# Finding the first expert's rows without the lists, and building the job table beside its products

## The chip, the cores and the metric

The kernel runs on one core of one Trainium2 chip. The metric is the device time of one launch in microseconds, taken as the median of several runs. The profile is of one further execution.

## What is computed

One decoder layer for 512 prompt rows and 8 sample rows, 1024 wide: an input projection, three mixers (pooling, dilated attention, a convolution), an output projection and a layer norm, then a mixture of 32 experts of which each row takes four, and a second layer norm. The part that matters here:

```python
logits = jnp.einsum('md,de->me', xt, router_w, ...) + router_b
top_v, top_i = lax.top_k(logits, TOP_K)          # 4 of 32
gates = jax.nn.softmax(top_v, axis=-1)
...
def run_block(args):                             # rows of one expert
    hh = xblk @ e_w_in[e] + e_b_in[e]
    gate, up = jnp.split(hh, 2, axis=-1)
    ...
    act = gate * jax.nn.sigmoid(SWIGLU_ALPHA * gate) * (up + 1)
    return act @ e_w_out[e] + e_b_out[e]
```

and the sum of the results per row, weighted by the gates. All is float32.

## The kernel before, in words

`layer` runs two blocks one after the other; each block ends with a barrier of all engines, and each has its own program for SyncE, GpSimd, ScalarE, TensorE (PE) and VectorE.

**first_block** does everything up to the router. The prompt rows are four tiles of 128, worked in the order 3, 2, 1, 0 (`TILES`), and the sample rows are a fifth tile, NT, which comes first (`NTH` is the place of a tile in that order). `AFTER` is an order written out by hand: which product of which tile stands at which step of the attention. For each tile VectorE normalises the rows (`shifted1`, `scaled1`), ScalarE stores them to `x1_dram` and `acc_dram` (`x1_store`, L759), PE computes the logits (`logits`), VectorE takes the four best experts (`choose_experts`, called by `route`) into the 0/1 table `memb`, PE counts with 0/1 products how many earlier rows chose the same expert (`rank`), and VectorE turns the rank into a place (`place_in_lists`, L1438). GpSimd scatters row number and gate to that place in `lists_dram` (`list_rows`, L656, four indirect DMAs a tile). After the last tile VectorE builds the job table from the totals (`job_table`, L1566, with two rounds through PE: `placed_ready` to `ordered`, and `fields_ready` to `fields_turned`) and writes it to `jobs` (`job_rows`, L1613). When all scatters have landed (`listed`), SyncE and ScalarE load the lists to SBUF (L622 to L626, L840 to L842). Then the block ends.

**moe_block** works off jobs. A job is up to five groups of 32 rows of one expert; the most frequent expert comes first but for expert 0, which a constant puts ahead of all. Expert weights stream through `ring`, twelve slots of 1 MB: eight hold the up and gate weights, four the down weights. The slots of expert 0 are loaded in first_block. In moe_block SyncE loads the next expert's unit k into its slot as soon as the product that reads it is done (`load_unit`, L278; `wait_ge(up_done, ...)`, L1727 on). For each job GpSimd gathers the rows (`gather`, L1776), VectorE turns them (`turn_rows`, L2000), PE does `up` (L1856) and, one job later, `down` (L1874), VectorE and ScalarE the activation, ScalarE `results` (L1935), and GpSimd scatters the results with an addition onto `acc_dram` (`scatter`, L1785). VectorE's `name_rows` (L1989) takes a job's gates and indices from the lists, which the gather needs; for jobs 0, 1 and 2 it stands ahead of the loop, with memsets of the PSUM tiles `pu` and `py` (L2014, L2015). At the end GpSimd waits for all scatters and signals `sums_done` (L1838), on which SyncE loads the sums for the second layer norm (L1748).

## Time and profile before

| what | us |
|---|---|
| median of 3 runs (lowest, highest) | 1352.47 (1349.94, 1352.83) |
| the profiled execution | 1353.31 |
| its span, first to last instruction | 1351.5 |
| PE busy | 1180.6 (87%) |
| VectorE busy | 515.6 (38%) |
| ScalarE busy | 272.9 (20%) |
| GpSimd busy | 244.6 (18%) |
| mean GB/s over the span | 343 |
| mean granted TensorE clock | 0.952 |

The span ends with the last instruction; the 1.8 us around it belong to the launch. Shares of busy time are means over stages with different limits: first_block ends at about 286 us, and moe_block takes the rest. The page shows the span in 40 slices of 33.8 us. In a timeline a line stands for neighbouring instructions of one kind; the time in brackets is how long the engine was idle before it, with what ended that. "issue" is time in which the engine waited for nothing that the profile shows. PEld is the load of weights into the array, SPq, ACTq and POOLq are the sequencers that issue DMAs.

### The profile page before, as it was taken

To read this page: it belongs to the slowest core of one execution; us is meant where nothing else is said; L and a number is where in the kernel's file an instruction comes from. 1 tells how busy PE (TensorE), PEld (TensorE's weight loads), DVE (VectorE), ACT (ScalarE), POOL (GpSimd) and SP (SyncE) were. 2 spreads that over 40 slices of the span, in tenths; PEclk is the share of its full clock that TensorE was granted. 3 is DMA by queue.
4 is the path that set the end of the run, shared out by engine and by line. 5 is a ranking of instruction groups with operands and counts; after the bars stand their busy time and mean duration, and the time that the engine had idled before them with its cause. 6 is when DMAs were issued, how large, how long until landed. Compare 5 with 4: busy or idle time off the path is not lost.

```text
span 1351.5 us, 34174 instructions
## 1 busy us (share of the span) xinstructions
PE 1180.6 (87%) x12540; PEld 521.5 (39%) x12541; DVE 515.6 (38%) x875; ACT 272.9 (20%) x533; POOL 244.6 (18%) x214
## 2 busy tenths in 40 slices
PE   7998999836999999999899989989898989998750
PEld 6886545512333333433233333433333333433210
DVE  2997637854232222232324141421323220422226
ACT  0003234400102230141121211130121210132212
POOL 4000001431111221142121311221121212130112
PEclk9999999958899999999999999999999999999765
DMA  9702931649999999999999999999999999999943
GB/s 356 201 3 97 289 146 34 261 152 414 416 419 411 409 413 381 419 385 413 417 410 416 409 413 413 409 404 418 416 407 415 410 419 363 409 403 422 412 177 128
DMA packets 79976, 463.18 MB, mean 343 GB/s; under 512 B 12324, under 2 KB 20873, under 8 KB 29709
## 3 DMA queue, kind: packets, MB, share of 16 engines
q1 hardware_dynamic: 69083, 438.76, 80.3%
q0 software_dynamic: 8768, 17.47, 5.1%
q10 hardware_dynamic: 2066, 6.32, 1.2%
q8 instruction: 18, 0.29, 0.1%
q14 instruction: 41, 0.34, 0.1%
HBM read 447.51 MB, written 19.48 MB: 346 GB/s over the span
## 4 chain that ended last, share of the span: by engine, by line
PE 51%; DMA 21%; issue 3%; DVE 2%; ACT 0%; DVEq 0%; ACTq 0%; POOLq 0%; SPq 0%; POOL 0%
PE pu L1866 32%; PE rest L1880 17%; DMA ring<-in_e_in 15%; DMA ring<-in_e_out 6%; PE pu L1860 1%; PE rest L1891 1%; DVE fin L2082 0%; DVE bn L2064 0%; DVE xgT L2003 0%; DVE mv L2075 0%; PE rest L1885 0%; ACT y L1946 0%; DMA fin<-acc_rows 0%; DVE idx L1995 0%; ACT fin L1977 0%
## 5 line engine op out<-in xcount | busy, mean ns | idle before, releaser
L1866 PE MATMUL pu<-ring,xgT 128*32 128x512 f32 x5248 | 587.6, 601 | 37.8 <-DMA ring<-in_e_in 37.1
L1866 PEld LDWEIGHTS pu<-ring,xgT 128*32 128x32 f32 x5248 | 162.2, 111 | 445.3 <-issue 444.7
L1880 PE MATMUL rest<-ring,hid 128*32 128x256 f32 x5248 | 301.5, 387 | 20.1 <-DMA ring<-in_e_out 11.8
L2033 DVE TENSOR_SCALAR gg<-pu 128x1280 f32<-128x1280 f32 x32 | 47.7, 1492 | 607.2 <-PE pu L1866 607.2
L1789 POOL DMA_INDIRECT acc_rows<-y,row x82 | 110.7, 1350 | 748.0 <-ACT y L1946 731.8
L1880 PEld LDWEIGHTS rest<-ring,hid 128*32 128x32 f32 x5248 | 168.4, 112 | 143.0 <-issue 41.3
L1946 ACT ACTIVATE y<-rest,gate 32x256 f32 x328 | 152.8, 466 | 292.8 <-issue 289.1
L1926 ACT ACTIVATE ss<-gg 128x1280 f32<-128x1280 f32 x32 | 40.7, 1272 | 540.5 <-DVE gg L2033 540.5
L866 PE MATMUL pair<-xt,ring 128*128 128x260 f32 x448 | 101.7, 389 | 6.9 <-DMA ring<-in_w_in 5.8
L1779 POOL DMA_INDIRECT xq<-x_rows,idx x82 | 88.2, 1075 | 90.0 <-issue 78.2
L866 PEld LDWEIGHTS pair<-xt,ring 128*128 128x128 f32 x448 | 86.4, 194 | 21.0 <-DMA xt<-in_xT 6.8
L1210 DVE SCALAR_TENSOR_TENSOR conv<-conv,chan_sb 128x512 f32<-128x512 f32 x90 | 67.7, 752 | 3.1
L1860 PE MATMUL pu<-brow,chosen 128*32 128x512 bf16 x328 | 25.8, 413 | 40.9 <-issue 29.3
L2003 DVE STREAM_TRANSPOSE xgT<-xq 128x1280 f32<-128x1280 f32 x33 | 49.7, 1506 | 0.0
L2045 DVE TENSOR_TENSOR uu<-uu,ss 128x1280 f32<-128x1280 f32 x32 | 47.7, 1492 | 1.1
L2050 DVE STREAM_TRANSPOSE hid<-uu 128x1280 f32<-128x1280 f32 x32 | 48.1, 1504 | 0.0
L2048 DVE CAST chosen_down<-cst 128x32 bf16 x32 | 5.8, 181 | 109.7 <-PE rest L1880 106.8
L2043 DVE SCALAR_TENSOR_TENSOR uu<-uu,gg 128x1280 f32<-128x1280 f32 x32 | 47.6, 1486 | 0.0
L2035 DVE TENSOR_SCALAR uu<-pu 128x1280 f32<-128x1280 f32 x32 | 47.4, 1481 | 0.0
L662 POOL DMA_INDIRECT list_rows<-pairs,spots x20 | 21.1, 1055 | 126.1 <-DVE spots L1453 121.6
L1003 PE MATMUL pair<-ring,mix 128*128 128x512 f32 x80 | 39.7, 647 | 0.0
L1860 PEld LDWEIGHTS pu<-brow,chosen 128*32 128x32 bf16 x328 | 6.8, 99 | 60.0 <-issue 57.9
(270 smaller groups left out, 542.3 us busy)
## 6 DMA issues: line engine op xcount, KB each, us to landing
ring<-in_e_in SPq DMA_DIRECT2D x256, 1024.0 KB, 23.9
ring<-in_e_out SPq DMA_DIRECT2D x128, 1024.0 KB, 25.1
ring<-in_w_in SPq DMA_DIRECT2D x3, 1536.0 KB, 24.5
ring<-in_w_in SPq DMA_DIRECT2D x5, 512.0 KB, 11.0
ring<-in_w_o SPq DMA_DIRECT2D x1, 2048.0 KB, 12.0
conv<-in_x_prompt SPq DMA_DIRECT2D x1, 2048.0 KB, 13.8
x_rows<-conv ACTq DMA_DIRECT2D x4, 512.0 KB
acc_rows<-conv ACTq DMA_DIRECT2D x4, 512.0 KB
```

Source lines behind the costliest of these rows:

```text
L866: mm = nc.tensor.matmul(b[:, h, 0:HALF], wtile[:, tiles_of(lo, lo + P).start, k], xt[:, k, h * HALF:(h + 1) * HALF], start=k == 0, stop=k ...
L1210: ch.mark(V.scalar_tensor_tensor(cy[:, i, 0:SEQ], u[:, i, t:t + SEQ], taps[:, i, t:t + 1], cy[:, i, 0:SEQ], ALU.mult, ALU.add))
L1779: nc.gpsimd.indirect_dma_start(out=xq[:, u % 2, j], out_offset=None, in_=x1_quarters, in_offset=bass.IndirectOffsetOnAxis(ap=idx4[:, u % A ...
L1789: nc.gpsimd.indirect_dma_start(out=acc_dram, out_offset=bass.IndirectOffsetOnAxis(ap=row4[0:GS, u % AHEAD, j:j + 1], axis=0), in_=y[at, u ...
L1866: mm = nc.tensor.matmul(pu[quarter(c), j], xgT[:, j, k], w[:, :, c * QC:(c + 1) * QC], start=False, stop=k == KT - 1, skip_group_check=True)
L1880: mm = nc.tensor.matmul(py[quarter(c), j], hid[:, j, 2 * q + f], w[:, f, c * QC:(c + 1) * QC], start=False, stop=q == FT // 2 - 1 and f == ...
L1946: ins = nc.scalar.activation(y[to, bass.ds(u % 2, 1), j // NQ, c * QC:(c + 1) * QC].rearrange("p o n -> p (o n)"), py[of, j], ACT.Copy, sc ...
L2003: V.transpose(xgT[:, :, :, :].rearrange("p j k s -> p (j k s)"), xq[:, half].rearrange("p j n -> p (j n)")).then_inc(turned, 1)
L2033: V.tensor_scalar(gg[:, :, :], pu[:, :, 0], SW_LIMIT, None, ALU.min).then_inc(g_ready, 1)
L2043: at.do(V.scalar_tensor_tensor(uu[:, :, :], uu[:, :, :], 1.0, gg[:, :, :], ALU.add, ALU.mult))
L2045: V.tensor_tensor(uu[:, :, :], uu[:, :, :], ss[:, :, :], ALU.mult).then_inc(h_ready, 1)
L2050: V.transpose(hid[:, :, :, :].rearrange("p j f s -> p (j f s)"), uu[:, :, :].rearrange("p j n -> p (j n)")).then_inc(hid_ready, 1)
```

## The change

The lists, job table and expert stream are as they were, but the first job no longer needs them.

- **The first expert's rows.** For every tile VectorE makes a 0/1 table of row against slot, `in_slot`, from the rank for expert 0 (`first_slots`, two operations). PE multiplies it with the row numbers, split in two bf16 parts (`first_ids_of`): 80 products for the tiles NT, 3, 2 and 1, ahead of `logits(0)`, and 20 for tile 0 behind the totals. VectorE adds the two and writes the first job's indices `idx4[:, 0]`, and the first job's size `first_size` from the totals. GpSimd gathers the rows (`gather_first`) within first_block, after a wait for all stores of the rows. `next_expert` tells SyncE which expert follows.
- **What moves.** The scatter of tile 0's list entries goes from the end of first_block to the head of moe_block; the loads of the lists go to ScalarE's queue in moe_block (eight loads); the rest of `job_table` and `job_rows` go to VectorE in moe_block, behind `turn_rows(0)`, and the four products that turn the fields stand in the middle of the first `up` (`turn_fields`). `jobs_ready` is a new semaphore on which SyncE, GpSimd, ScalarE, PE and VectorE wait before they read `jobs` or `count`. PE's first `up` stands ahead of its loop.
- **Memory.** `pu`, `rest`, `pairs`, `spots`, `idx4`, and `qkv` (under which `xq`, `xgT` and `hid` now lie) belong to both blocks. The PSUM memsets go to VectorE's head in first_block, with a wait on PE's first use of each bank. The zero fills of `xq` on ScalarE and GpSimd go, since the memory holds finite numbers. Small tables move into `cpre`, which is free by then.
- **The end.** SyncE waits for the count of scatters itself; `sums_done` goes.

The core of the diff:

```diff
@@ first_block, gpsimd
-            for i in (NT,) + TILES:
+            for i in (NT,) + TILES[:-1]:
                 list_rows(i, NTH[i])
+            gp.wait_ge(x1_sent, 32 * (NT + 1))
+            gp.wait_ge(first_named, 1)
+            size = gp.value_load(first_size[0:1, 0:1], min_val=1, max_val=JG)
+            x1_quarters = x1_dram.rearrange("r (c n) -> (r c) n", n=QC)
...
+            gather_first(0)
@@ first_block, tensor
+            def first_ids_of(tiles, dst):
+                pe.wait_ge(slots_ready, NTH[tiles[-1]])
+                for j in range(JG):
+                    for i in tiles:
+                        m = rows(i)
+                        for c in range(NQ):
+                            mm = nc.tensor.matmul(dst[c * GS:(c + 1) * GS, j], in_slot[0:m, i, j * GS:(j + 1) * GS],
+                                                  id_parts[0:m, i], start=i == tiles[0], stop=i == tiles[-1],
+                                                  skip_group_check=True)
+                mm.then_inc(ids_done, 1)
...
             turn_rows1(0)
+            pe.wait_ge(s_max, 2 * NSTEPS)
+            first_ids_of((NT,) + TILES[:-1], ids_early)
             logits(0)
             rank(0)
-            pe.wait_ge(s_max, 2 * NSTEPS)
...
+            pe.wait_ge(ids_kept, 1)
+            first_ids_of((0,), ids_last)
@@ first_block, vector
+            for b in pair:
+                V.memset(b[:, :, :], 0.0).then_inc(psum_zero, 1)
+            for b in bS + bT:
+                ch.mark(V.memset(b[:, :], 0.0))
...
+            def first_slots(i, ranks):
+                m = rows(i)
...
+                ch.do(V.scalar_tensor_tensor(keys[0:m, i:i + 1], ranks[:, 0:1], 1.0, memb[0:m, i, 0:1], ALU.add, ALU.mult))
+                V.tensor_scalar(in_slot[0:m, i], C("slot", m), keys[0:m, i:i + 1], None, ALU.is_equal
+                                ).then_inc(slots_ready, 1)
...
             scaled1(1)
+            d.wait_ge(ids_done, 1)
+            V.tensor_copy(early_ids[:, :, :], ids_early).then_inc(ids_kept, 1)
             root1(0)
             shifted1(0)
             route(0)
             scaled1(0)
+            d.wait_ge(rank_done, NTH[0] - 1)
+            d.wait_ge(m_ready, NTH[0])
+            first_slots(0, ranks_of(0))
...
+            V.tensor_scalar(idx4[:, 0], first_ids[:, :, 0], float(NQ), C("quarterpad"), ALU.mult, ALU.add
+                            ).then_inc(first_named, 1)
@@ moe_block, sync
-            first = expert_of(1)
+            first = sp.value_load(next_expert[0:1, 0:1], min_val=0, max_val=NE - 1)
...
+            sp.wait_ge(jobs_ready, 1)
...
-            sp.wait_ge(sums_done, 1)
+            done = sp.value_load(jobs[0:1, 4, bass.ds(last, 1)], min_val=1, max_val=JG * MAXJ)
+            sp.wait_ge(scattered, 16 * done)
@@ moe_block, scalar
-            nc.scalar.activation(xq[:, 0]...).then_inc(xq_zero, 1)
+            a.wait_ge(listed, 16 * TOPK * (NT + 1))
+            for c in range(NQ):
+                a.dma_start(lists[c * GS:(c + 1) * GS, 0:NE * JG], lists_dram[:, 0:NE * JG]).then_inc(lists_in, 16)
+            for c in range(NQ):
+                a.dma_start(lists[c * GS:(c + 1) * GS, NE * JG:], lists_dram[:, NE * JG:]).then_inc(more_lists_in, 16)
@@ moe_block, vector
+            choose(0)
+            turn_rows(0, d.value_load(first_size[0:1, 0:1], min_val=1, max_val=JG))
+            job_table()
+            job_rows()
+            d.wait_ge(jobs_ready, 1)
             d.wait_ge(lists_in, 16 * NQ)
             name_rows(ch, 0, 0)
-            choose(0)
-            ch.mark(V.memset(pu[:, :, :, :], 0.0))
-            ch.mark(V.memset(py, 0.0))
             d.wait_ge(more_lists_in, 16 * NQ)
             for u in (1, 2):
                 name_rows(ch, u, d.value_load(jobs[0:1, 2, u:u + 1], min_val=0, max_val=NE * MAXN - 1))
-            turn_rows(0, through(slice(1, 2)))
```

## Rows read from the trace of the kernel before

**Rows 1.** the page, slices of 33.8 us: DMA share, GB/s.

```profile
DMA  9702931649999999999999999999999999999943
GB/s 356 201 3 97 289 146 34 261 152 414 416 419 411 409 413 381 419 385 413 417 410 416 409 413 413 409 404 418 416 407 415 410 419 363 409 403 422 412 177 128
```

**Rows 2.** window: PE, PEld, DVE, ACT, POOL busy us; granted clock, DMA share, GB/s.

```profile
1200.00:1250.00 50.00, 44.47 (x550) 16.36 (x542) 18.26 (x22) 10.00 (x18) 4.18 (x5) 1.00 1.02 415
```

**Rows 3.** DMA issues: queue, count, KB each, us to landing.

```profile
ring<-in_e_in SPq DMA_DIRECT2D x256, 1024.0 KB, 23.9
...
rw<-in_router_w ACTq DMA_DIRECT2D x1, 128.0 KB, 21.2
...
l2b<-in_ln_b SPq DMA_DIRECT2D x1, 512.0 KB, 16.3
```

**Rows 4.** timeline (start us, us, engine, line), the stream's start.

```profile
294.74 1.04 PE L1860 MATMUL pu<-brow,chosen 128*32 128x512 bf16 x8 [11.57 <-DVE xgT L2003]
...
298.70 12.31 SPq L281 DMA_DIRECT2D ring<-in_e_in  x8
...
318.69 7.92 SPq L281 DMA_DIRECT2D ring<-in_e_in  x8
```

**Rows 5.** the columns of rows 2, in the gap.

```profile
278.00:280.00 2.00, 0.00 (x0) 0.00 (x0) 1.77 (x16) 0.00 (x0) 0.99 (x2) 0.50 0.10 30
```

**Rows 6.** timeline, a PSUM memset and PE's first product.

```profile
287.32 2.19 DVE L2014 MEMSET pu<- 128x2560 f32 x1 [0.53 <-issue]
...
5.59 3.81 PE L866 MATMUL pair<-xt,ring 128*128 128x260 f32 x8 [5.59 <-DMA ring<-in_w_in]
```

**Rows 7.** timeline, VectorE from last projection to job fields.

```profile
262.70 1.28 DVE L1411 TENSOR_TENSOR conv<-conv,pair 128x512 f32<-128x512 f32 x2
...
268.43 0.25 DVE L1418 SCALAR_TENSOR_TENSOR lg<-route_sums,mv,pair 128x32 f32<-128x32 f32 x1
...
275.70 0.19 DVE L1581 COPY xt<-bS 128x32 f32<-128x32 f32 x1 [0.77 <-PE bS L1181]
...
281.04 0.21 DVE L1610 TENSOR_SCALAR xt<-xt 128x1 f32<-128x1 f32 x1
```

**Rows 8.** the columns of rows 2, in the attention part.

```profile
200.00:250.00 50.00, 48.68 (x255) 27.24 (x254) 36.75 (x129) 19.29 (x59) 7.54 (x8) 1.00 0.22 77
```

**Rows 9.** timeline, grouped form and window: small products.

```profile
264.88 1.94 PE L1052 MATMUL pair<-rw,xt 128*128 128x32 f32 x16 [0.18 <-ACT xt L797]
...
270.89 0.42 PE L1174 MATMUL bS<-memb,tri_bf 128*32 128x32 bf16 x5
...
L1174 PE MATMUL bS<-memb,tri_bf 128*32 128x32 bf16 x4 | 0.3, 193 | 0.0
...
270.00:272.00 2.00, 1.08 (x15) 0.84 (x15) 1.93 (x5) 0.00 (x0) 0.00 (x0) 0.57 1.00 268
```

**Rows 10.** timeline, the last store of the rows.

```profile
272.07 0.95 ACTq L763 DMA_DIRECT2D acc_rows<-conv  x1
```

**Rows 11.** timeline and window, gathers to the first turn.

```profile
286.17 1.27 ACT L1952 ACTIVATE xq<-cst 128x1280 f32<-128x1280 f32 x1 [16.37 <-PEq L325]
...
288.36 1.06 POOL L1779 DMA_INDIRECT xq<-x_rows,idx  x1 [9.06 <-ACT xq L1952]
...
290.00:292.00 2.00, 0.00 (x0) 0.00 (x0) 2.00 (x7) 0.00 (x0) 1.63 (x2) 0.50 0.29 78
...
292.33 1.51 DVE L2003 STREAM_TRANSPOSE xgT<-xq 128x1280 f32<-128x1280 f32 x1
```

**Rows 12.** timeline, chain and window at the stream's end.

```profile
1316.35 1.32 POOL L1789 DMA_INDIRECT acc_rows<-y,row  x1 [8.94 <-ACT y L1946]
...
1318.97 3.05 issue
...
1323.99 2.14 SPq L1714 DMA_DIRECT2D fin<-acc_rows  x5
...
1318.00:1319.00 1.00, 0.00 (x0) 0.00 (x0) 0.00 (x0) 0.00 (x0) 0.00 (x0) 0.50 0.28 37
```

342 lines of the change are left out of this document (198 added, 144 removed).

## The prediction

> **What bounds the kernel now.** I read the page's slices first. From the ninth slice (270 to 304 us) on, the DMA row stands at 9 and the GB/s row near 412 until the last two slices [rows 1]. A stretch of 50 us says the same more finely: DMA share 1.02 at 415 GB/s, while PE is busy 44 of 50 us [rows 2]. What is streamed is fixed: the page's list of DMA issues gives 256 units of 1 MB for the up weights, eight per expert [rows 3], and the down weights are four more per expert, 384 in all. The first expert's twelve come before this stretch; the other 372 need a slot that a product has emptied. So the kernel is: a first part that ends with the first unit of expert products, then a saturated stream whose length is bytes over rate, then a tail. What moves the start of the stream moves its end by as much, as long as the stream never runs dry; what makes an engine faster inside it is worth nothing.
>
> Next I read the place where the stream starts. PE begins the first up product at 294.74, SyncE issues its first unit at 298.70 (3.96 later), and the next eight units at 318.69 [rows 4]. [...]
>
> **Parts with one answer.** The PSUM memsets move to the head of VectorE: 2560 columns took 2.19 us, 0.86 us per thousand, so 4096 columns cost some 3.6 us from 0.3 to 4 us; PE's first product starts at 5.59, held by its DMA [rows 6]. Nothing, with 1.6 us to spare; without that cover it would cost up to 3.6. The zero fills of xq on ScalarE and GpSimd go: worth nothing of their own, as the path is built anew below. The two operations of first_slots for each of the tiles NT, 3 and 2 (some 0.5 us a tile, twice the 0.25 of L1418 [rows 7]) lie beside PE, which is busy 48.68 of 50 us where VectorE is busy 36.75 [rows 8]; between 0 and 1.5, I take 0.3. The constants grow by 171 columns (88 KB) and no early wait is on them.
>
> **The front, step by step.** From PE's last projection on, VectorE leads. I shift the old times.
> 1. first_slots(1) stands ahead of rest_sum(0), which started at 262.70: +0.5. turn_rows1(0) on PE, done at 264.7, is done at 265.2 [rows 7].
> 2. 80 new products (5 groups, 4 tiles, 4 quarters) of 32 weight columns and 2 moving columns stand on PE ahead of logits(0). The nearest row is L1174, five products of 32 weight columns in 0.42 us; one alone takes 0.19, so each further one 0.055 [rows 9]. 80 x 0.055 = 4.4, so 269.6. Bounds: 0.19 each (15.2 us), if none overlaps, and 0.028 each (2.2 us), if the spacing halves with the clock, which was granted at 0.57 in that window [rows 9]. I take the row as it stands.
> 3. logits(0) took 1.95 [rows 9]: 271.55. VectorE copies the early numbers and runs root and shift (1.3) beside it. route(0) starts at 271.65 and not at 268.43: +3.2 [rows 7].
> 4. scaled1(0) ended at 271.67, now 274.9. first_slots(0) 0.5, 20 products 1.2, three chained operations 0.65: the indices of the first expert are there at 277.4.
> 5. GpSimd first waits for the stores of x1 and acc_rows. The last was issued at 272.07 (0.95 long) [rows 10]; now 3.2 later, until 276.2. With it the DMA engines were busy until 278 and fell to 30 GB/s then [rows 5]; a store issued until 276.2 lands at 279.0 by my choice (bounds 277.5, where the old ones had ended, and 281). This wait ends later than step 4, so it is the one that decides.
> 6. GpSimd starts a gather 0.9 after its releaser (ScalarE's fill ended at 287.44, the gather started at 288.36), and the second follows 1.36 later: 279.9 to 282.3. In the old kernel the gathered bytes moved within 290:292, right behind the issues [rows 11]; landed by 283.5.
> 7. The block ends with GpSimd. VectorE ended at 285.36 and its first operation of the next block was at 286.33: +1.0, 283.3. Its memset, choose and one value load take 1.0, the turn of the rows 1.5, PE's start 0.9 (293.84 to 294.74) [rows 4, 11]: PE starts at 286.7 and not at 294.74. **Front: -8.0** (bounds -10.0 and +5.4, by steps 2 and 5). VectorE's other work ahead of the block's end (tables, weigh, place: 1.3 + 2.1 + 0.4 after 277.4) ends at 281.2, 1.1 before GpSimd; that is its cover.
>
> **What is moved behind the start.** The job table takes 275.70 to 281.25 [rows 7]; it now starts at 285.8 and its fields are there at 291.3. PE has four units behind it at 295.6 (the old first up ended at 310.47 and the last four of its eight units took 6.9, so they began 8.9 after its start; 286.7 + 8.9), so it does not wait; the four turning products add 1.9 us (281.31 to 283.17), jobs_ready is at 299.6, and the first up ends at 304.4. Queued behind: the four list scatters of tile 0, 4 x 1.29 after 283.3, landed at 289.7; then eight loads on ScalarE's queue, issued until 293.2. They land within 2 us in a quiet machine (issued 280.50 to 283.24, the bytes gone by 285); with SyncE's queue full a small load on ScalarE's queue took 21.2 (rw, at the start of the kernel) [rows 3]. I take 5: VectorE is at name_rows until 303.1, the second job's gather lands near 307, and VectorE can turn it at 304.4 + 3.0. The second up starts 5.7 after the first ends, as before, at 310.1, its first unit is issued at 312.6, 21.9 us after the stream's first (before: 20.0). The queue holds eight units and the LN2 rows, which were issued at 311.53 and landed 16.3 later [rows 3], 29.1 us after the first issue. The stream has 7.2 us of slack there and nothing is lost, save the bytes: 640 KB of lists (four loads of 40 KB, four of 120) now share the stream, 0 to 1.6 us at 412 GB/s; I take **+1.0**.
>
> [...]
>
> **The tail.** The last scatter is issued at 1316.35 (1.32 long). GpSimd then walks out of its unrolled loop: the chain shows two long stretches of "issue", the second of 3.05 us, and SyncE's first load of the sums is at 1323.99. The DMA windows have the scatter's bytes in 1318:1319 [rows 12] and almost nothing after 1320. With SyncE waiting on the scatters itself, it starts at about 1320.1: **-3.9** (bounds -5.5 and 0). Late next is nothing new: ScalarE's table was loaded at 1316.78, and GpSimd's first addition is wanted only at 1328.8.
>
> **Sum.** -8.0 + 0.3 + 1.0 - 3.9 = -10.6. The profiled execution took 1353.31 (span 1351.5), so 1342.7; it lies 0.84 above the median of 1352.47, so 1341.9 for a median.
>
> **Rivals.**
> - More gain (0.16): products at 0.028 us, stores landed at 277.5 and the other steps of the front a little shorter give -10.0, a scatter landed by 1318.5 gives -5.5, the lists nothing: 1337.3. For it: the clock is at its upper level when the 80 run; against it that other rows of this width have the same spacing at that level (54 products of L1880 in 3.23 us, though of 256 columns).
> - The lists come late (0.12). If the eight loads take the 21.2 us of rw, they land at 314, the second job's rows are turned at 321 and the stream's next issue is at 33.8 us, 4.7 after the queue is empty: 1346.6.
> - The tail gives nothing, since the accumulating scatter's own completion is what took until 1323 (0.12): 1345.8. For it: the chain cannot show when a semaphore was raised. Against it: the bytes.
> - The start moves but not the end, since some later stage refills the gap (0.05): only the tail is left, 1348.6. Against it the share of 1.0 throughout.
> - Slower (0.04): the small products do not overlap. At 0.19 us each, 100 of them cost 19 us where I have 5.6, all of it ahead of the router and of the x1 stores: +13.4 - 10.6 = +2.8, 1355.3 for a median. The sum turns at 0.16 us a product.
> - The change does what it says by its code; I give no case to the contrary.
>
> **How the numbers follow.** Forecast 0.51, 1340 to 1344.5. To hold 8 in 10 the range takes in the larger gain and the two middle losses: 1337 to 1348. A measurement of this kernel tells 0.2% (2.7 us) from no change. Faster by more: forecast, more gain, lists, tail and most of the fourth case, 0.92. Within 0.2%: 0.04, the fourth case with a small loss. Slower: 0.04.
>
> **What would show it.** In the profile after: the first up product near 286.7, SyncE's first unit near 290.7; 80 products in about 4.4 us and logits(0) behind them; GpSimd's first gather near 279.9, released by a DMA and not by VectorE; the first up with a pause of about 2 us in its middle; DMA share 1.0 without a hole 25 to 35 us after the first unit; SyncE's loads of the sums some 2.5 us after the last scatter's issue and not 6.3. The prediction is wrong if the stream has a hole there, if the gather waits for something later than the stores, or if the new products take 0.1 us or more.

## The result: slower by 0.3%

The changed kernel took 1355.7 us as the median of 14 runs (1353.57 to 1360.36), the kernel before 1352.8 us on the same chip: a ratio of 1.003, with a 95% interval of 1.0019 to 1.0042. The forecast was faster by 10.6 us. In the profiled executions the spans are 1352.3 us after and 1351.5 before. Here and below, a difference in us is the ratio times the median of the kernel before, and intervals go the same way; the two medians can lie apart by another amount, here by 2.9 us where the ratio says 4.1. Two executions of the kernel with the tail change alone, at 2484.76 and 1444.74 us, count as slow and stand in no ratio.

The page after, the rows that answer to [rows 1] (DMA share and GB/s of 40 slices), and the windows that answer to [rows 2] and [rows 5], with one more in a place that becomes important:

```profile
DMA  9703930749999998999999999999999999999953
GB/s 356 203 3 111 298 124 34 272 168 403 415 418 412 408 412 330 417 376 411 418 409 415 410 412 413 407 409 412 416 408 414 410 418 383 392 406 420 412 221 128
```

```profile
278.00:280.00 2.00, 0.00 (x0) 0.00 (x0) 0.00 (x0) 0.00 (x0) 0.00 (x0) 0.50 0.00 0
520.00:540.00 20.00, 20.00 (x219) 6.51 (x215) 2.23 (x2) 0.70 (x1) 0.00 (x0) 1.00 0.76 282
1200.00:1250.00 50.00, 46.59 (x574) 17.34 (x566) 18.25 (x22) 7.67 (x13) 6.92 (x6) 1.00 1.02 410
```

The sixteenth slice stands at 330 GB/s where it was 381: a hole in the stream. In 520:540 it is 282 GB/s, where the kernel before moved 371, and PE is busy in all 20 us, within a job of 320 products. The waits of PE in the changed kernel (engine, line, what for: us in total, times, longest), first all of those in 370:620, then the longest group in 620:1310:

```profile
PE pu L1882 <- issue: 7.9, 8, 1.8
```

```profile
PE pu L1888 <- DMA ring<-in_e_in: 34.8, 34, 2.2
```

Up to 620 us PE never waits for a load of weights (in the kernel before twice, 1.1 us in all). Behind that it does, again and again.

The front of the changed kernel, as a timeline (start, duration, engine, line, operation, idle time before it and what ended that):

```profile
263.92 1.47 PE L1045 MATMUL pu<-cpre,ktok 8*32 8x2 bf16 x80
265.32 3.49 PE L1095 MATMUL pu<-rw,xt 128*128 128x32 f32 x16
268.91 0.25 DVE L1464 SCALAR_TENSOR_TENSOR cpre<-cpre,mv,pu 128x32 f32<-128x32 f32 x1 [1.15 <-PE pu L1095]
...
272.56 0.45 ACTq L797 DMA_DIRECT2D acc_rows<-conv  x1
...
273.57 0.23 DVE L1637 TENSOR_SCALAR idx<-cpre,cst 128x5 int32<-128x5 f32 x1
...
280.53 1.06 POOL L698 DMA_INDIRECT qkv<-x_rows,idx  x1 [11.92 <-issue]
...
286.35 0.18 DVE L2028 CAST chosen<-cst 128x32 bf16<-128x32 f32 x1 [9.03 <-PEq L346]
...
289.39 1.04 PE L1882 MATMUL pu<-brow,chosen 128*32 128x512 bf16 x8 [13.64 <-DVE qkv L2044]
...
293.64 0.35 SPq L301 DMA_DIRECT2D ring<-in_e_in  x1
```

So the start did move: PE's first up product from 294.74 to 289.39 and SyncE's first unit from 298.70 to 293.64 [rows 4], 5.1 to 5.4 us earlier. Then the head start is lost. The second and third up product of the changed kernel:

```profile
307.58 0.17 DVE L2034 COPY gate<-lists 128x5 f32 x1 [5.47 <-DMA lists<-list_rows]
...
309.55 1.05 POOL L1801 DMA_INDIRECT qkv<-x_rows,idx  x1 [18.01 <-DVE idx L2036]
...
315.81 1.51 DVE L2044 STREAM_TRANSPOSE qkv<-qkv 128x1280 f32<-128x1280 f32 x1 [0.79 <-DMA qkv<-x_rows,idx]
...
318.13 0.62 PE L1882 MATMUL pu<-brow,chosen 128*32 128x512 bf16 x4 [11.60 <-DVE qkv L2044]
318.52 8.67 PE L1888 MATMUL pu<-ring,qkv 128*32 128x512 f32 x56
330.21 1.86 PE L1888 MATMUL pu<-ring,qkv 128*32 128x512 f32 x8 [3.02 <-issue]
...
347.95 0.83 PE L1882 MATMUL pu<-brow,chosen 128*32 128x512 bf16 x12
```

and the same of the kernel before:

```profile
316.16 0.62 PE L1860 MATMUL pu<-brow,chosen 128*32 128x512 bf16 x4 [5.69 <-issue]
316.56 9.53 PE L1866 MATMUL pu<-ring,xgT 128*32 128x512 f32 x64
...
343.00 1.51 PE L1860 MATMUL pu<-brow,chosen 128*32 128x512 bf16 x12
```

The second up product starts 2.0 us later than before instead of 5.4 earlier, and takes until 332.1 with a pause of 3.02 us ahead of its last eight products; the third starts 4.95 us later. VectorE reads the first product at 312.04, 5.5 us after it ended; in the kernel before it does so at once. The last scatter's issue is 4.5 us later too (1320.84 against 1316.35 [rows 12]), and the tail gives about that back:

```profile
1320.84 1.31 POOL L1811 DMA_INDIRECT acc_rows<-y,row  x1 [9.95 <-ACT y L1984]
1324.27 2.60 SPq L1734 DMA_DIRECT2D fin<-acc_rows  x5
```

SyncE loads the sums 3.43 us after the scatter's issue where it took 7.64 [rows 12].

Two theories go into the experiments. **P**: TensorE's chain, from the second up product to about 615 us, decides, and the stream has slack until then; the hole at 520 us is where its head start goes. **S**: the stream's start decides, as forecast. What made the second and third up products late is a question of its own, with three suspects: the lists, the second job's gather, and TensorE's code.

### The profile page after: what moved, and what is told of

The parts are those of the page before. It is cut to its first block, busy times and chain, and to the rows that moved or that the text cites. A ratio compares the mean times of both kernels' runs of the same rounds, so it can differ in the third digit from the quotient of the medians.

```text
span 1352.3 us, 34408 instructions
## 1 busy us (share of the span) xinstructions
PE 1182.7 (87%) x12640; PEld 524.3 (39%) x12641; DVE 519.2 (38%) x900; ACT 271.9 (20%) x532; POOL 242.8 (18%) x213
## 4 chain that ended last, share of the span: by engine, by line
PE 50%; DMA 23%; issue 3%; DVE 2%; ACTq 0%; ACT 0%; DVEq 0%; POOL 0%; SPq 0%; POOLq 0%
PE pu L1888 31%; PE rest L1904 16%; DMA ring<-in_e_in 14%; DMA ring<-in_e_out 8%; PE pu L1882 1%; DMA lists<-list_rows 1%; PE rest L1915 1%; DVE fin L2185 0%; DMA qkv<-x_rows,idx 0%; DVE bn L2167 0%; DVE mv L2178 0%; DMA fin<-acc_rows 0%; DMA acc_rows<-y,row 0%; DMA list_rows<-pairs,spots 0%; PE rest L1909 0%
## 5 line engine op out<-in xcount | busy, mean ns | idle before, releaser
L1888 PE MATMUL pu<-ring,qkv 128*32 128x512 f32 x5248 | 592.9, 605 | 38.1 <-DMA ring<-in_e_in 34.8
L1888 PEld LDWEIGHTS pu<-ring,qkv 128*32 128x32 f32 x5248 | 165.1, 111 | 445.8 <-issue 442.8
L1904 PE MATMUL rest<-ring,qkv 128*32 128x256 f32 x5248 | 299.2, 386 | 17.0 <-DMA ring<-in_e_out 11.0
L1904 PEld LDWEIGHTS rest<-ring,qkv 128*32 128x32 f32 x5248 | 167.6, 111 | 139.3 <-issue 35.5
L898 PE MATMUL pu<-xt,ring 128*128 128x260 f32 x448 | 101.1, 388 | 7.8 <-DMA ring<-in_w_in 6.0
L1801 POOL DMA_INDIRECT qkv<-x_rows,idx x80 | 86.2, 1077 | 95.1 <-issue 64.9
L898 PEld LDWEIGHTS pu<-xt,ring 128*128 128x128 f32 x448 | 85.9, 192 | 21.8 <-DVEq L1239 5.2
L2044 DVE STREAM_TRANSPOSE qkv<-qkv 128x1280 f32<-128x1280 f32 x33 | 49.7, 1506 | 1.7 <-issue 0.9
L2153 DVE STREAM_TRANSPOSE qkv<-uu 128x1280 f32<-128x1280 f32 x32 | 48.2, 1505 | 0.0
L1035 PE MATMUL pu<-ring,mix 128*128 128x512 f32 x80 | 39.7, 647 | 0.0
```

The lines of the kernel that those rows point to most:

```text
L898: mm = nc.tensor.matmul(b[:, h, 0:HALF], wtile[:, tiles_of(lo, lo + P).start, k], xt[:, k, h * HALF:(h + 1) * HALF], start=k == 0, stop=k ...
L1801: nc.gpsimd.indirect_dma_start(out=xq[:, u % 2, j], out_offset=None, in_=x1_quarters, in_offset=bass.IndirectOffsetOnAxis(ap=idx4[:, u % A ...
L1888: mm = nc.tensor.matmul(pu[quarter(c), j], xgT[:, j, k], w[:, :, c * QC:(c + 1) * QC], start=False, stop=k == KT - 1, skip_group_check=True)
L1904: mm = nc.tensor.matmul(py[quarter(c), j], hid[:, j, 2 * q + f], w[:, f, c * QC:(c + 1) * QC], start=False, stop=q == FT // 2 - 1 and f == ...
L2044: V.transpose(xgT[:, :, :, :].rearrange("p j k s -> p (j k s)"), xq[:, half].rearrange("p j n -> p (j n)")).then_inc(turned, 1)
L2153: V.transpose(hid[:, :, :, :].rearrange("p j f s -> p (j f s)"), uu[:, :, :].rearrange("p j n -> p (j n)")).then_inc(hid_ready, 1)
```

## Experiment: the tail alone, and the front alone

```diff
+            done = sp.value_load(jobs[0:1, 4, bass.ds(last, 1)], min_val=1, max_val=JG * MAXJ)
+            sp.wait_ge(scattered, 16 * done)
-            sp.wait_ge(sums_done, 1)
...
-            gp.sem_inc(sums_done, 1)
```

> The kernel before with nothing but the change in the tail: SyncE waits for the two scatters of the row sums itself, and GpSimd's own signal is gone. In the changed kernel the load of the sums was issued 3.43 us after the last scatter's issue, against 7.64 us before. If that saving is one of the wait's form, this kernel has it too and is 4.2 us faster than the kernel before (about 1348.6 us). If the scatter's own landing set the 7.64 us, or if the saving only swallows a wait of later work, it is within 0.5 us of the kernel before.

Measured: ratio 0.9942 (0.9919 to 0.9965), 7.8 us, more than expected. The same kernel was run again, and with it the changed kernel with the old tail:

> The kernel before with the tail change alone, once more: its ratio was 0.9942 (0.9919 to 0.9965), 7.8 us, where its profile shows 4.2 us. If the 4.2 us are all, the ratio comes out near 0.9969; if there is more in it, near 0.994 again.

Measured: 0.9968 (0.9955 to 0.9982), 4.3 us. In its profile the last scatter is issued at 1315.60 and the load of the sums at 1318.89, 3.29 us later.

> The changed kernel with the old tail: GpSimd signals SyncE that the scatters are done. If the profiles size the parts rightly (tail -4.2 us, front +4.5 to +7 us), it is 4.2 us slower than the changed kernel and 7 us slower than the kernel before, near 1360 us, and the load of the sums is issued 7.6 us after the last scatter's issue again. If the tail alone is worth the 7.8 us that its kernel showed by the clock of whole runs, it is 10 to 12 us slower than the kernel before.

Measured: 1.0057 (1.0037 to 1.0077), 7.7 us slower than the kernel before. Its profiled execution was the fastest of its six runs (1354.36 us, median 1358.73), and has the scatter at 1317.70 and the load at 1325.37: 7.67 us, the old tail. The medians are only 4.8 us apart, so the size of this loss is the least certain of the three.

So the halves are: **tail -4.3, front +7.7 us** against forecasts of -3.9 and -6.7. They add up to +3.4, and +0.3% is +4.1. The first measurement of the tail alone, from five executions, was high, as the second and the profiles say. The rest is about the front.

## Experiment: the stream starts later

```diff
@@ moe_block, sync, the first eight units
-                sp.wait_ge(up_done, k + 1)
+                sp.wait_ge(up_done, min(k + 3, KT))
```

> The changed kernel, with the first eight loads that SyncE issues of the weight stream put behind one more of TensorE's up products each than they wait for now, so that the stream starts about 4 us later. Theory P (TensorE's chain from the second up product to about 615 us decides, and the stream has slack): the holes of the stream between 500 and 550 us shrink by about what it starts later, and the time is within 0.5 us of the changed kernel. Theory S (the stream's start decides, as the prediction said): about 3.7 us slower than the changed kernel, some 1359 us.

Measured: 1353.56 us, ratio 0.9999 (0.9987 to 1.0012), where the changed kernel had 1.003: not slower, but faster by some 4 us (by the medians against the kernel before, 2.7). The first unit is issued at 297.41 and not at 293.64. The window at the hole:

```profile
520.00:540.00 20.00, 20.00 (x243) 7.33 (x239) 5.38 (x8) 1.27 (x1) 0.00 (x0) 1.00 0.92 363
```

The hole has shrunk from 282 to 363 GB/s. Theory S is refuted: 3.8 us taken from the stream's start cost nothing. That it gained was not expected by either theory. The trace shows where: with less of the stream under way (208 GB/s in 296:300 where the changed kernel moved 375), the list loads of 120 KB land 3.2 us after their issue and not 8.3, VectorE's wait for the second part of the lists is 1.39 us and not 5.47, and the second up product starts at 314.89 instead of 318.13.

```profile
303.83 0.17 DVE L2034 COPY gate<-lists 128x5 f32 x1 [1.39 <-DMA lists<-list_rows]
```

## Experiment: row names ahead of the second part of the lists

```diff
-            d.wait_ge(more_lists_in, 16 * NQ)
             for u in (1, 2):
                 name_rows(ch, u, ...)
+            d.wait_ge(more_lists_in, 16 * NQ)
             ch.wait()
```

The wait is VectorE's.

> The changed kernel, with GpSimd's... and TensorE's wait for the second part of the job lists moved behind the row names of jobs 1 and 2, whose entries for these rows lie in the part that lands first. The names of job 1 then no longer wait the 5.47 us for lists. Theory P (TensorE's chain from the second up product decides): the second up product starts about 4.3 us earlier (near 313.8 instead of 318.1 us) and the time is about 4.3 us below the changed kernel's, near 1351.4 us. Theory S (the stream decides): the second up product is earlier and the time is unchanged.

Measured: 1353.93 us, ratio 0.9999 (0.9985 to 1.0013), again some 4 us below the changed kernel. The second up starts at 313.75; but the first started 2.3 us earlier in this execution (287.12), so that the distance between the two shrank only from 28.74 to 26.63 us. The names of job 1 are there at 300.9 and its gather is issued at 302.42, 7.1 us earlier; GpSimd goes on at 310.06, 6.6 us after it was through with the issue, and VectorE turns the rows at 311.53. But VectorE is not free of the lists. The wait that was moved now stands ahead of its first read of the product, which ended at 304.1:

```profile
308.57 1.49 DVE L2136 TENSOR_SCALAR gg<-pu 128x1280 f32<-128x1280 f32 x1 [6.76 <-issue]
```

The view of the loads of the second part (L1994) names who waited for them:

```profile
  DVE gg L2136: 6.8, 1
```

The last of these loads has landed at 305.38, and the chain has four lines of VectorE's sequencer (DVEq, from 305.38 to 308.15) ahead of 308.57. From 308.57 to the turn at 311.53 VectorE is never idle, and the gather has landed before it. So the lists are one cause of the loss, this edit takes only a part of it away, and the gather stands right behind them. A kernel in which VectorE reads the first product ahead of this wait was not tried.

## Experiment: only TensorE's first up product written out

```diff
@@ moe_block of the kernel before, tensor
+            size = pe.value_load(jobs[0:1, 5, 0:1], min_val=1, max_val=JG)
+            pe.wait_ge(turned, 1)
+            pe.wait_ge(chosen_ready, 1)
+            pe.wait_ge(pu_read, 1)
+            up(size, 1)
             last = job_count(pe)
...
+                    with pe.If(step > 1):
-                    with pe.If(step <= last):
+                        with pe.If(step <= last):
```

> The kernel before, with the code of TensorE's first up product written out ahead of the loop, as the changed kernel has it, so that the loop's own up code runs first for the second job. No operation is added or removed. Theory of code that is met for the first time: the second up product shows the pause of about 3 us that the changed kernel has inside it (327.19 to 330.21), takes 12.5 to 14 us instead of 9.9, and the kernel is 2.5 to 3 us slower than before. Rival (the pause comes from the data of the second job, or from elsewhere): second up as before, time within 0.5 us.

Measured: 1360.09 us, ratio 1.0043 (1.0027 to 1.0059), 5.8 us slower than before, twice what was expected, with every operation the same. This is a cause that the prediction did not have at all. The timeline of the profiled execution, which was the slowest of its twelve (1362.8 us):

```profile
317.91 0.62 PE L1860 MATMUL pu<-brow,chosen 128*32 128x512 bf16 x4 [7.06 <-issue]
318.54 4.44 PE L1866 MATMUL pu<-ring,xgT 128*32 128x512 f32 x24
324.69 3.19 PE L1866 MATMUL pu<-ring,xgT 128*32 128x512 f32 x25 [1.71 <-issue]
330.54 1.92 PE L1866 MATMUL pu<-ring,xgT 128*32 128x512 f32 x15 [2.66 <-issue]
...
352.05 1.22 PE L1860 MATMUL pu<-brow,chosen 128*32 128x512 bf16 x12
```

The second up product has two pauses, of 1.71 and 2.66 us, and takes 14.5 us from bias to end instead of 9.9. The pauses are put down to "issue": PE waited for nothing that the profile knows.

The DMA tables of narrow windows show packets beside them. The profile lists a queue `q8` of the kind "instruction", with packets of 16 KB: 18 in the whole kernel before (0.29 MB), 21 in the changed one and 21 here (0.34 MB). Stepping through in windows of 1 us, packets of this queue stand in 318:319, 330:331, 337:338 and 342:343 in the kernel before, and in 319:320, 322:323, 327:328, 334:335, 341:342 and 347:348 here. Those of 322:323 and 327:328 stand where the two pauses above begin (322.98 to 324.69 and 327.88 to 330.54), and the two long ones of the down product behind them (3.53 us until 336.49, 3.16 until 349.68) have one inside. In the changed kernel packets stand in 321:322, 327:328, 333:334 and 340:341, and its pauses are from 327.19 to 330.21, 335.06 to 336.27 and 338.74 to 342.72. The kernel before has such pauses too, in its first down product, 2.73 us until 333.15 and 3.68 until 339.58, each with one of the packets named; what the written-out copy adds are those in the second up product. Not every packet goes with a pause: those of 318:319 before, 319:320 here and 321:322 in the changed kernel have none beside them. Two stretches around the second up product, 318:332 of the changed kernel and 316:330 of the kernel before, as sums by queue kind:

```profile
q8 instruction: 2, 0.03, 0.9%
```

```profile
q8 instruction: 1, 0.02, 0.5%
```

The author's reading is that with the first up product in the loop PE's second one runs code that was read for the first, and that written out ahead it leaves the loop's own copy to be read when the stream is running (407 GB/s in 322:331 here). That `q8` carries TensorE's code is inferred from the agreement in time alone; the profile names no engine for it.

## Experiment: the same code, but no stream beside it

```diff
@@ the kernel of the last experiment, sync, head of the loop over u
+                with sp.If(u < 2):
+                    sp.wait_ge(down_done, FT)
```

> The kernel before with the first up product written out ahead of the loop, and SyncE holds the loads of the third up product until the first down product is done, so that from about 320 us, when the second's loads have landed, no transfer of the stream runs. If the pauses in the second up product and in the first down product (2.66, 3.53 and 3.16 us in the same kernel with the stream) come from reading new code behind the stream's transfers, those behind 320 us fall under 1.5 us each. If reading new code takes this long on its own, they stay at 2.5 to 3.7 us. The total says nothing here: the third up product waits for its loads.

Measured, in the one execution of this kernel:

```profile
324.39 5.25 PE L1870 MATMUL pu<-ring,xgT 128*32 128x512 f32 x40 [1.64 <-issue]
...
331.72 3.66 PE L1884 MATMUL rest<-ring,hid 128*32 128x256 f32 x64 [1.60 <-issue]
335.74 2.78 PE L1884 MATMUL rest<-ring,hid 128*32 128x256 f32 x42 [0.35 <-issue]
338.85 1.50 PE L1884 MATMUL rest<-ring,hid 128*32 128x256 f32 x22 [0.33 <-issue]
```

From 330 to 340 us the DMA share is 0.02. The packets of `q8` are there as well (in 329:330, 333:334, 336:337 and 339:340), but the three waits of the down product, 3.53, 0.70 and 3.16 us with the stream, are 1.60, 0.35 and 0.33 without. Two are as expected and the first is 0.1 us above the bound of 1.5. So the long pauses fit the reading of new code behind the stream's transfers, and most of their length is the stream's. The pause of 1.64 us in the up product still lay beside it (324.39; the DMA share in 320:330 is 0.63).

## Experiments: the first up product back in the loop

The first try puts the first job's size into the loop's first word ahead of the job table, leaves the first two passes of the loop empty, and puts `turn_fields` behind a condition in the loop's up code:

```diff
-            size = pe.value_load(first_size[0:1, 0:1], ...)
...
-            up(size, 1, turn_fields)
-            pe.wait_ge(jobs_ready, 1)
-            last = job_count(pe)
             with pe.Fori(0, NWORD) as w:
+                with pe.If(w > 0):
+                    pe.wait_ge(jobs_ready, 1)
                 word = pe.value_load(jobs[0:1, 0, bass.ds(w, 1)], ...)
                 with pe.Fori(0, 3) as i:
-                    step = 3 * w + i + 1
+                    step = ((3 * w + i + 62) & 63) + 1
```

> The changed kernel with TensorE's first up product back in the loop: its size stands in the loop's first word ahead of the job table, the transposes of the job table stand behind a condition inside the loop's up code, and the guards read the sizes. The same products run; only where their code lies is changed, besides two branches for each job. Theory C (code met for the first time while the weight stream runs costs pauses of about 3 us): the second up product takes about 9.5 us instead of 13.9, the third starts 4 to 4.5 us earlier (near 343.5 us against 347.95), and the time is about 4 us below the changed kernel's, near 1351.5 us. Rival (the pause belongs to the second job's data or the late row names): second up as in the changed kernel, time within 1 us of it.

Measured: 1361.77 us, ratio 1.0069 (1.0048 to 1.009), a miss by 10 us, and an instructive one:

```profile
301.82 1.04 PE L1883 MATMUL pu<-brow,chosen 128*32 128x512 bf16 x8 [23.65 <-issue]
...
326.23 0.62 PE L1883 MATMUL pu<-brow,chosen 128*32 128x512 bf16 x4 [7.72 <-DVE qkv L2044]
326.63 9.77 PE L1889 MATMUL pu<-ring,qkv 128*32 128x512 f32 x64
```

The second up product is as it should be (9.77 us, no pause). But PE's first product is 12.4 us late. Some 2.2 us of it were there before the passes (the first of the 80 small products stands at 266.16 and not at 263.92), and PE's wait ahead of the up product is 10.0 us longer (23.65 against 13.64): the empty passes jump over all of the up and down code, and packets of `q8` stand in 291:292, twice in 294:295 and in 299:300 before it starts. The kernel with early row names besides came out likewise:

> Both repairs of the changed kernel: first up product back in the loop, and the row names of jobs 1 and 2 ahead of the wait for the second part of the lists. If the two losses are separate (late names 4.3 us, new code 4 us), the second up product starts near 314 us and the third near 340 us, 3 us before the kernel before's 343.0; with the tail's 4.2 us and the third up product's lead this gives 1345 to 1347 us. If they overlap, the third starts near 343 us and the time is about 1349 us.

1.0091 (1.0066 to 1.0117), and with the later stream besides:

> As the kernel with both repairs, and the first eight loads of the weight stream about 4 us later. Theory P (TensorE's chain decides and small transfers of the second job suffer from the stream): the second up product starts 1 to 3 us earlier than without, the time is the same or up to 2 us less. Theory S (the stream's start decides once TensorE is early enough): 2 to 4 us more than without.

1.0117 (1.0081 to 1.0153). Both rest on a first up product near 290 and say nothing on their own question; they started it at 299.99 and 298.15.

The second try starts the inner loop at the first job's pass and works out the step number once:

```diff
-                with pe.Fori(0, 3) as i:
-                    step = ((3 * w + i + 62) & 63) + 1
+                with pe.Fori(word >> 12, 3) as i:
+                    step = pe.snap(((3 * w + i + 62) & 63) + 1)
```

> As the first kernel with the up product back in the loop, without its two empty passes ahead of the first up product (the inner loop now starts at the pass of the first job) and with the step number worked out once for each job. In that kernel TensorE sat 23.65 us ahead of its first product and not 13.64, and 2.1 to 2.3 us instead of 0.6 us ahead of each later up product. If the empty passes (jumps over code that was never read) made the first and the repeated arithmetic the second, then the first up product starts near 289.4 us again, the later ones after about 0.6 to 0.8 us, the second up product has no pause (9.8 us), the third starts near 343 to 344 us and the time is 3 to 5 us below the changed kernel's, near 1351.5 us. If a jump of about 3 us stays, the first up product starts at 292 to 293 us.

Measured: 1353.76 us, ratio 1.0003 (0.9991 to 1.0015), 0.27% below the changed kernel. The first half came out to the microsecond:

```profile
288.95 1.04 PE L1883 MATMUL pu<-brow,chosen 128*32 128x512 bf16 x8 [13.58 <-DVE qkv L2044]
...
317.75 9.52 PE L1889 MATMUL pu<-ring,qkv 128*32 128x512 f32 x64
...
341.18 1.47 PE L1883 MATMUL pu<-brow,chosen 128*32 128x512 bf16 x12 [0.62 <-issue]
```

No packet of `q8` moves between 317 and 327 (the changed kernel had one in 321:322), and the third up product starts 6.8 us earlier than in the changed kernel. But the next eight jobs give 5.7 us back: from the end of the third up product to the up product near 600 us it takes 238.6 us (363.53 to 602.14), against 232.9 in the changed kernel (369.37 to 602.23) and 231.9 before (365.52 to 597.40). The loss stands at every third job: 2.2 to 2.3 us ahead of the up product instead of 1.6 to 1.8, and 22.5 us for 192 products instead of 20.8.

With the early row names besides:

> The same with the row names of jobs 1 and 2 ahead of the wait for the second part of the lists. Second up product near 314 us, third near 339 to 341 us. With the tail's saving this gives 1345 to 1348 us if each loss is separate; if the third up product is held by the pauses of the first down product, as in the kernel before, it is 1348 us, the time of the kernel with the tail change alone.

Measured: 0.9982 (0.9967 to 0.9997). Its front started late in the profiled execution (290.40), and the third up product at 340.90.

What the loss at every third job is, was asked with two more:

```diff
-                with pe.If(w > 0):
-                    pe.wait_ge(jobs_ready, 1)
+                pe.wait_ge(words_ready, w + 1)
```

> As the loop kernel with early row names, and the condition at each word of the loop (two branches) replaced by a wait on a counter that is always met later. In that kernel the wait ahead of every third up product was 2.2 to 2.3 us against 1.6 to 1.8 in the changed kernel, and the up product behind it took 22.5 us instead of 20.8 (192 products) and 35.7 instead of 34.5 (320 products). If the condition's jump makes these, they return to 1.7, 20.8 and 34.5 us, eight jobs take 233 us again instead of 238.6, and the time is 4 to 5 us lower, near 1346.5 us. If the place of the code in the instruction memory makes them, they stay, or move to other jobs, and the time changes by under 2 us.

Measured: 1348.73 us, ratio 0.9969 (0.9956 to 0.9982). The wait is 1.9 us, the 320 products take 34.51 again, the 192 behind the first backward jump 21.92, and the eight jobs 235.9 us: a part of the loss goes with the condition, not all of it. VectorE still waits here for the second part of the lists, ahead of its first read of the product:

```profile
309.71 1.49 DVE L2137 TENSOR_SCALAR gg<-pu 128x1280 f32<-128x1280 f32 x1 [6.89 <-issue]
```

```diff
-            with pe.Fori(0, NWORD) as w:
+            with nc.Fori(0, NWORD, engines=OrderedEngineSet([pe.engine]), hint_back_edge=True) as w:
```

> The same with the option of the outer loop that announces its backward jump. [...]

Measured: 0.9987 (0.9974 to 1.0001): no gain; the wait is 2.1 to 2.2 us, the 192 products are back at 20.81, and the 320 take 35.93. Between 380 and 600 us no packet of `q8` moves in any of these kernels, so if those packets are TensorE's code, this loss is not the reading of it. What it is stays open.

## Experiment: the code at another place

```diff
@@ the changed kernel with early row names, tensor
-            with pe.Fori(0, NWORD) as w:
+            with nc.Fori(0, NWORD, engines=OrderedEngineSet([pe.engine]), head_slot={pe.engine: 0}) as w:
```

> [...]

Measured: 1353.96 us, ratio 1.0006 (0.9993 to 1.0018). In the kernel with early row names, without the option, the second up product has its pauses after 32 and 56 products (0.78 and 2.96 us) and the first down product after 26 and 64 (0.54 and 3.78). The places moved: the first up product has a pause of 0.95 us now, PE sits 13.56 us ahead of the second (it starts at 321.06 and then runs 9.70 us without a pause), and the down product's pauses of 2.24, 1.86 and 2.39 us stand ahead of its bias, after 32 and after 96 products. The products and their data are the same, so the pauses do not belong to the data. That they go with the code's place is what is left; no view shows where the code lies.

## Experiment: a condition around each job

```diff
@@ the kernel before, tensor, in the loop
+                    with pe.If(step > 0):
-                    with pe.If(step <= last):
+                        with pe.If(step <= last):
```

> The kernel before with one more condition, always true, around what TensorE does for each job, as the changed kernel has it. The wait ahead of each up product should grow by the 0.12 us by which it is longer in the changed kernel (1.77 against 1.66 us, 0.64 against 0.52 us), so that eight jobs between 366 and 600 us take 232.9 instead of 231.9 us. Theory C expects no new pause inside the second up product and at most 1 us on the total. If the condition itself made the pause, the second up product would take 13 us or more.

Measured: 1.0 (0.9987 to 1.0012). Both profiles have 34174 instructions, so the condition, which always holds, seems to have been dropped on the way to the chip. So the run says nothing about a condition, and is one more of the kernel before. As such it is useful: its third up product starts at 340.28 and its last scatter is issued at 1314.43, where the profile of before has 343.00 and 1316.35. One profile is good to 2 or 3 us here.

## One table for the chain

Theory P can be read across the profiled executions: start of the stream, start of TensorE's third up product, start of the up product near 600 us, issue of the last scatter.

| kernel | first unit | third up | up near 600 | last scatter |
|---|---|---|---|---|
| a condition around each job (= before) | 296.66 | 340.28 | 593.50 | 1314.43 |
| tail alone | 297.67 | 340.14 | 593.39 | 1315.36 |
| tail alone, again | 297.08 | 341.38 | 595.70 | 1315.60 |
| loop, names, counter | 292.41 | 339.34 | 596.62 | 1315.01 |
| before | 298.70 | 343.00 | 597.40 | 1316.35 |
| names early | 291.49 | 344.47 | 598.76 | 1317.49 |
| front alone | 291.75 | 344.82 | 599.07 | 1317.70 |
| loop, names, counter, hint | 294.08 | 341.08 | 599.58 | 1317.74 |
| stream later | 297.41 | 344.83 | 599.11 | 1318.48 |
| loop, second try, names | 294.80 | 340.90 | 601.39 | 1319.44 |
| loop, second try | 293.03 | 341.18 | 602.14 | 1319.62 |
| changed kernel | 293.64 | 347.95 | 602.23 | 1320.84 |
| names early, code at another place | 293.71 | 347.99 | 602.24 | 1321.38 |
| first up written out | 299.09 | 352.05 | 607.18 | 1325.47 |
| loop, first try, names, stream later | 305.85 | 348.39 | 608.54 | 1326.90 |
| loop, first try, names | 304.15 | 349.63 | 609.97 | 1328.61 |
| loop, first try | 305.87 | 351.01 | 611.50 | 1328.91 |

From 597 us on the last column follows the one before it: from the row of the kernel before to that of the first up written out 9.1 us, where that has 9.8, and to the last row 12.6, where that has 14.1. It does not follow the first: starts of 291.49 and 297.41 us end within 1.0 us of each other. Below about 597 us the end no longer follows the chain either (593.39 and 596.62 give the same end to 0.4 us): there something else takes over. Starts that differ by 5 us make no difference there either. What it is stays open: behind 620 us PE waits for the stream's up units 25 to 36 times in each of five kernels, the kernel before and the changed one among them, so the stream's rate is a candidate, but it was not tried by itself. The four profiles of the old front have a mean of 595.0 and the two of the new one as it was predicted (changed kernel and front alone) 600.7; 5.7 us is the front's loss in this view, 7.7 in the timed runs.

## Why the prediction was wrong

**The step that failed is the first, "What bounds the kernel now".** A DMA share of 1.02 in 1200:1250 [rows 2] and nines in the slices [rows 1] were read as one saturated stream from 300 us on, so that whatever moves its start moves its end and what an engine does inside it is worth nothing. Up to about 615 us it is the other way round. PE waits for no load of weights from 370 to 620 us (7.9 us of "issue" are all that it waits), and in 520:540, where a job of 320 products holds the slots, the stream waits for PE: 282 GB/s. The stream's start 3.8 us later cost nothing. The row was on the page: slice 16 has 381 GB/s before. The rival "the start moves but not the end, since some later stage refills the gap" had the mechanism, with a chance of 0.05; even it had no loss in it.

**Step by step.**
- Memsets at the head: nothing, right (they end at 5.2 us, PE starts at 5.52).
- 80 products: 4.4 us forecast, 1.47 measured, 0.018 each. The row of five products had 32 moving columns where these have 2, and was too far away: the measured time lies below all that the prediction weighed, 15.2, 4.4 and 2.2 us. The rival of 0.19 us each is refuted by the same row; that its 1355.3 us is 0.4 from the measured median is luck. But `logits(0)` behind them took 3.49 us and not 1.94, in a stretch with a granted clock of 0.51 (265.4:268.8; 0.50 from 265.6 on), where the kernel before had run the same products in 264:266 at 1.00. Together the detour is 4.96 us against the 6.35 assumed, and the route started only 0.5 us later than before, not 3.2.
- Indices of the first expert: 277.4 forecast, 273.8 measured; the last store of the rows issued at 272.56, not 275.3.
- GpSimd's gather: 279.9 forecast, 280.53 measured, although the indices were 3.6 us earlier and the stores 2.7. In 278:280 no engine works and the DMA queues move one packet of 0.00 MB, so the stores' bytes are through. In 280:281 the profile has a packet of the instruction queue `q14`. That GpSimd was reading code is likely by analogy and was not tried.
- Block end: +1.0 forecast. From the end of the second gather's issue (282.93) to VectorE's first operation it is 3.4 us. With turn and start PE is at 289.39 instead of 286.7.
- So the front moved the start by 5.35 us where 8.0 were forecast: right in kind, mis-sized by GpSimd's two waits, which more than used up what the products gave.
- Lists: landed within 5 us by forecast; the wait for the second part lasted until 307.58, and the chain of waits has 9.70 us for these loads. This term was mis-sized, though the loads did not take the 21.2 us of the rival either. The early names showed it as one cause, by 2 us in the distance of the two up products and 4 us in the time, with VectorE's 6.8 us of waiting for the lists still there.
- The second job's gather: landed near 307 by forecast, 6.2 us after its issue at 309.55 in the trace.
- "The second up starts 5.7 after the first ends": 11.60 measured. Here the text said that the stream has 7.2 us of slack and that nothing is lost. The slack was real, and worthless, since the stream was not what counted.
- TensorE's code: not in the text at all. The first up product was written out ahead of the loop; alone, that costs 5.8 us (3.6 to 8.0), the largest single loss measured by itself. With it back in the loop, its side costs gone as far as they went, and the early names, the kernel is at 0.9969.
- Tail: -3.9 forecast, -4.2 in the profile, -4.3 (-6.1 to -2.4) in the timed runs. Right, and by the reason given: the scatter's bytes had landed, and GpSimd's way out of its loop was the delay. The rival "the tail gives nothing" is refuted.

The sum is then: tail -4.3; the front alone +7.7 (5.0 to 10.4), made of a written-out product that costs 5.8 alone and a late second job of which the early names gave back 4, less whatever the earlier start is worth. These do not add up to a sum of their own: they overlap, each has a wide interval, and how the 7.7 us divide was not measured.

**Against both kernels.** The kernel before with the tail change alone is the fastest here with the least effort: 1348.83 us, 0.9968, and 0.9942 when first timed. The whole change with early names, the product in the loop and the counter is level with it at 1348.73 us, 0.9969: the early front, as far as it was repaired, brings nothing on top of the tail. Its first up product starts at 288.40 where the tail kernel's starts at 293.21, but its second at 314.48 against 314.20: the head start is gone by then, in VectorE's wait for the lists, and near 600 us this kernel is 0.9 us behind. Whether an early front without that wait would bring something is not shown, and below 597 us the end may not follow the chain (see the table).

## What to carry to other kernels

A DMA share of 1.0 in one window (here 1.02 at 415 GB/s in 1200:1250) does not make the whole stage stream-bound (here 0.76 at 282 GB/s in 520:540 of the changed kernel): look for the slices below it, and ask at several places who waits for whom, before pricing a head start at its full worth. The place of code can cost time with every operation the same: here one product written out ahead of its loop cost 5.8 us (3.6 to 8.0), with pauses of 1.71 and 2.66 us in the loop's first pass while the stream ran at 407 GB/s; with the product back in the loop, the second up product ran without a pause (9.52 us). So let a loop's first pass fall before the stream, and count the copies of unrolled code. When a wait is moved, ask the trace what it now stands in front of. Price each half of a mixed change by a kernel of its own; here the good half hid more than half of what the other cost.

## What the runs showed of the hardware

- The DMA table lists a queue `q8` of the kind "instruction" with packets of 16 KB; 21 of them against 18 in a kernel of 1350 us came with a difference of 0.4% (`peeled` against before). Under a stream of 407 to 421 GB/s such a packet went with a pause of TensorE of up to 4.0 us (3.98 until 342.72 in the changed kernel) and at times with none, at 5 GB/s (330:340 of `peeled_quiet`) with pauses of 0.33 to 1.60 us. That the packets are TensorE's code is inferred from the times.
- Two passes of a loop without work, which jump over code not yet executed, came with 10.0 us more of waiting ahead of TensorE's first up product (23.65 against 13.64), and with four packets of `q8` in it.
- 80 products of 32 weight columns and 2 moving columns took 1.47 us, 0.018 us each, at a granted clock of 1.00 (263.9:265.4); the next 16, 128 by 32 in f32, took 3.49 us, nearly all of it at 0.50 (265.6:268.8), where they had taken 1.94 at 1.00 before (264:266).
- Small loads of 120 KB on ScalarE's queue took 8.3 us beside the stream and 3.2 with the stream started 3.8 us later; a gather of one group took 6.2 to 6.6 us.
- With one more condition for each third job in TensorE's loop, the up products behind it took 1.2 to 1.7 us longer (35.73 against 34.51 and 22.50 against 20.81), with no packet of `q8` from 380 to 600 us. Without the condition one of the two was still 1.1 us longer (21.92). It is not explained.
